# Delta-rule mixer of a decoder step: gate distances on ScalarE, an earlier block inverse, and sample slots in two periods

## What is computed

```
gc = cumsum(g);  decay = exp(gc_i - gc_j) for i >= j, else 0
A = (beta k) k^T * decay below the diagonal;  T = A + I;  solve T u = beta v, T w = beta k exp(gc)
v_new = u - w S;   o = (q exp(gc)) S + (q k^T * decay) v_new
S = S exp(g_last) + (k exp(g_last - gc))^T v_new
```

## Time and profile before

| | us |
|---|---|
| median of 3 runs (3142.27 to 3144.38) | 3142.46 |
| the profiled execution | 3141.53 |
| its span, first to last instruction | 3139.9 |
| PE busy in the span | 3018.0 |
| DVE busy | 1911.0 |
| ACT busy | 1349.6 |
| POOL busy | 186.7 |

### The profile page before, as it was taken

One profiled execution on the slowest core, in us unless ns is written; L12 is line 12 of the kernel. 1 busy time (PEld: TensorE's weight loads), 2 busy tenths in 40 slices (PEclk: granted clock), 3 DMA queues, 4 the chain that ended last, 5 costly groups with the idle time before them and its releaser, 6 DMA issues.

```text
span 3139.9 us, 59809 instructions
## 1 busy us (share of the span) xinstructions
PE 3018.0 (96%) x24010; PEld 2901.5 (92%) x24010; DVE 1911.0 (61%) x2734; ACT 1349.6 (43%) x1970; POOL 186.7 (6%) x227
## 2 busy tenths in 40 slices
PE   6999999999889999999997999999999999999997
PEld 5789999998878999987796999999999999999997
DVE  4644336454676477666369888888888883322224
ACT  5443444334245464434356455555555543212222
POOL 0000000001253000010000000000000001000011
PEclk9999999999999999999998999999999999999998
DMA  7563223332206557886664433333343344433323
GB/s 260 166 214 108 81 76 88 93 94 71 68 28 196 166 183 255 275 322 218 247 207 132 125 120 114 120 114 117 114 120 120 116 128 149 135 96 97 99 93 129
DMA packets 455029, 443.96 MB, mean 141 GB/s; under 512 B 22203, under 2 KB 417740, under 8 KB 446879
## 3 DMA queue, kind: packets, MB, share of 16 engines
q1 hardware_dynamic: 436698, 361.85, 37.4%
q0 software_dynamic: 12416, 69.55, 6.1%
q10 hardware_dynamic: 5776, 10.62, 1.0%
HBM read 408.26 MB, written 33.95 MB: 141 GB/s over the span
## 4 chain that ended last, share of the span: by engine, by line
PE 85%; DVE 7%; ACT 3%; DMA 2%; issue 2%; POOL 1%; ACTq 0%; POOLq 0%; SPq 0%; DVEq 0%
PE ps L2931 17%; PE ps L3330 16%; PE ps L3534 15%; PE ps L3502 9%; PE ps L3504 9%; PE ps L3503 9%; PE ps L2928 4%; DVE w_low L1851 1%; ACT w_high L1118 1%; DMA w_raw<-in_xa_wo 1%; PE ps L3421 1%; DMA q_wide<-q_mid 1%; PE ps L2880 0%; PE ps L3147 0%; DMA w_raw<-in_xa_wk 0%
## 5 line engine op out<-in xcount | busy, mean ns | idle before, releaser
L1851 DVE TENSOR_TENSOR w_low<-w_raw,w_high 128x1024 fp32r<-128x1024 f32 x354 | 435.0, 1229 | 623.0 <-ACT w_high L1118 622.4
L3502 PE MATMUL ps<-set_high,w_hi 128*128 128x260 f32 x2464 | 700.9, 284 | 26.1 <-DVE set_low L2741 19.8
L3504 PE MATMUL ps<-set_high,w_lo 128*128 128x260 f32 x2464 | 700.0, 284 | 0.0
L3503 PE MATMUL ps<-set_low,w_hi 128*128 128x260 f32 x2464 | 699.9, 284 | 0.0
L1118 ACT ACTIVATE w_high<-w_raw 128x1024 fp32r<-128x1024 f32 x356 | 377.2, 1060 | 646.0 <-PE ps L3330 295.1
L3502 PEld LDWEIGHTS ps<-set_high,w_hi 128*128 128x128 f32 x2464 | 467.7, 190 | 29.6 <-DVE set_low L2741 22.6
L3504 PEld LDWEIGHTS ps<-set_high,w_lo 128*128 128x128 f32 x2464 | 468.7, 190 | 0.0
L3503 PEld LDWEIGHTS ps<-set_low,w_hi 128*128 128x128 f32 x2464 | 467.3, 190 | 0.1
L2931 PE MATMUL ps<-x_high,w_high 128*128 128x260 f32 x1568 | 319.7, 285 | 0.2
L2931 PE MATMUL ps<-x_low,w_high 128*128 128x260 f32 x1568 | 315.3, 283 | 0.0
L2931 PE MATMUL ps<-x_high,w_low 128*128 128x260 f32 x1568 | 314.8, 282 | 0.0
(11 more groups left out here) (532 smaller groups left out, 5582.7 us busy)
## 6 DMA issues: line engine op xcount, KB each, us to landing
w_raw<-in_w_in SPq DMA_DIRECT2D x96, 512.0 KB
raw<-in_ffn_w_up SPq DMA_DIRECT2D x176, 256.0 KB, 2.9
raw<-in_ffn_w_gate SPq DMA_DIRECT2D x176, 256.0 KB, 3.2
raw<-in_ffn_w_down SPq DMA_DIRECT2D x176, 256.0 KB, 3.0
w_raw<-in_w_out SPq DMA_DIRECT2D x64, 512.0 KB
w_raw<-in_xa_wq SPq DMA_DIRECT2D x64, 512.0 KB
w_raw<-in_xa_wo SPq DMA_DIRECT2D x64, 512.0 KB
w_raw<-in_xa_wk SPq DMA_DIRECT2D x32, 512.0 KB
```

The lines of the kernel that those rows point to most:

```text
L1851: dve.tensor_tensor(w_low[:, slot], w_raw[:, (g.slab0 + jj) % RAW], w_high[:, slot].bitcast(F32), ALU.subtract).then_inc(sem("w_low_ready" ...
L3502: pe.matmul(ps[:, bank, 0:HALF], high, set_high[:, kp, x], start=kp == 0, stop=False)
L3503: pe.matmul(ps[:, bank, 0:HALF], high, set_low[:, kp, x], start=False, stop=False)
L3504: ins = pe.matmul(ps[:, bank, 0:HALF], low, set_high[:, kp, x], start=False, stop=kp == KP - 1)
```

## The change

Gate distances: DVE's `differ` and `distance` go. ACT makes the absolute distance itself, straight from PSUM, one instruction per head (`far`, with the row's gate as bias and scale -1), and then the exponential as before. POOL clears `s_keys` in DVE's stead. The z GEMM's side work: the reciprocal of the norms goes ahead of a `w_low`; four single broadcasts become two pairs; the blocks' inverse starts one slab earlier and each of its pieces moves up one slab; `s_wide` is made at p = 10 and spread at the second quarter of slab 12, with a wait that ACT has taken block 2, and ACT takes it at p = 12. Chunks: `kk_of` goes to bank 4g, `samples_values` and `samples_step` move on DVE, `sample_keys_turn` goes behind `o_of`. Slots: (1, 0) to (1, 3) and (2, 0) to (2, 3), the first of each period in bank 4g+1. Tail: `o_turn(2)` goes to bank 4g ahead of `state_of`, and `chunk_done(2)` ahead of the last chunk's mean.

First the tables and the wait for `s_wide`, then ACT, then DVE's order in the loop over the chunks, then PE:

```
         WIDE = {(8, 1): (0, 1), (8, 2): (2, 3), (8, 3): (4, 5), (9, 0): (6, 7), (9, 1): (8,), (9, 2): (9,), (9, 3): (10,),
-                (10, 0): (11,), (10, 1): (12,), (10, 2): (13,), (10, 3): (14,), (11, 0): (15,)}
+                (10, 0): (11,), (10, 2): (12, 13), (11, 0): (14, 15)}
...
-        PAIR = {(n, x): u for u, (n, x) in enumerate((n, x) for n, xs in ((0, (4,)), (1, (1, 2, 3, 4)), (2, (1, 2, 3))) for x in xs)}
+        PAIR = {(n, x): u for u, (n, x) in enumerate((n, x) for n in (1, 2) for x in range(4))}
...
-        SLOT_AFTER = {1: ("grow", "differ"), 2: ("inner",), 3: ("k_rows",), 4: ("v_rows",)}
+        SLOT_AFTER = {0: ("inv_t6", 0), 1: ("far", 1), 2: ("far", 1), 3: ("k_rows", 1)}
...
+        def slot_bank(x, g):
+            return 4 * g + (3 if x else 1)
...
+                if p == 12:
+                    act.wait_ge(*after("s_wide_ready", 1))
+                    act.activation(s_bg[:, 0], ps[:, b, 0:BH], ACT.Copy)
+                    act.activation(s_bg[:, 1], ps[:, b, BH:2 * BH], ACT.Exp).then_inc(sem("s_bg_wide"), 1)
...
                 for g in (PREP if n == 0 else range(2)):
-                    act.wait_ge(*step("distance", g, n))
+                    act.wait_ge(*step("grow_ready", g, n))
+                    if n:
+                        act.wait_ge(*step("qk_mask", g, n - 1))
+                    for h in range(HG):
+                        m = n * H + g * HG + h
+                        ins = act.activation(decay[g][:, h], ps[:, 4 * g + 3, h * P:(h + 1) * P], ACT.Abs, bias=gc[:, m:m + 1], scale=-1.0)
+                    ins.then_inc(chunk_sem("far", g), 1)
+                    act.wait_ge(*step("far", g, n))
                     act.activation(decay[g][:], decay[g][:], ACT.Exp, scale=-1.0).then_inc(chunk_sem("decay", g), 1)
```

```
             for n in range(TT - 1):
                 if n:
                     less(n)
-                differ(n + 1)
-                distance(n + 1)
+                else:
+                    samples_values()
+                sample_states(n, 0)
                 if n == 0:
                     samples_taken()
-                    samples_step()
-                if n == 1:
-                    samples_done()
                 sample_states(n, 1)
                 inner_of(n + 1)
+                if n == 0:
+                    samples_step()
                 for g in range(2):
                     state(n, g)
...
                 inverse_of(5, n + 1)
                 if n == 0:
                     samples_rows()
+                if n == 1:
+                    samples_done()
...
-                if (p, k) == (ONE - 1, 1):
-                    pe.wait_ge(*normed(2 * H))
+                if (p, k) == (3 * SL, 1):
+                    pe.wait_ge(sem("acc_taken"), g_z.block0 + 3)
                     pe.wait_ge(*after("s_wide", 1))
...
                 if ahead:
-                    if n:
-                        samples_cleared(n - 1, 4)
+                    samples_beside(n, 0)
                     for g in range(2):
                         grow_of(n + 1, g)
...
                 for g in range(2):
                     v_new(n, g)
-                if ahead:
-                    samples_beside(n, 1)
...
+                samples_cleared(n, 0)
                 for g in range(2):
                     o_of(n, g)
                 if ahead:
-                    samples_cleared(n, 1)
+                    samples_beside(n, 1)
                     for g in range(2):
                         kk_of(n + 1, g)
+                else:
+                    for g in range(2):
+                        pe.wait_ge(*after("o_normed", 3))
+                        o_turn(2, g, 0).then_inc(sem("o_turned"), 1)
```

More of the change, by code:

```diff
@@ L3124, in half_of @@
                     pe.wait_ge(*step("inv_t0", g, n))
[L3125 removed]
+                    if n == 0:
+                        pe.wait_ge(*step("k_rows", g, n))
                 else:
```

155 lines of the change are left out of this document (66 added, 89 removed).

## The result

| | us |
|---|---|
| the changed kernel, median of 4 runs (3119.05 to 3125.4) | 3124.93 |
| before, median of 4 runs beside it (3142.27 to 3144.38) | 3143.22 |
| ratio, 95% interval | 0.9939 [0.9927, 0.9951] |
| the profiled execution, and its span | 3125.4, 3123.5 |
| forecast, and its range | 3123.8, 3118 to 3132 |

The kernel is 18.3 us faster by the medians, 0.6%, and lies inside the range. The profiled executions differ by 16.1 us. Where PE turns the gates' rows, ahead of anything that was changed, the new trace is at 717.73 and the old one at 716.57.

What follows compares the result with a forecast made beforehand. PE was taken to bound nearly everything, so gains up to the w_out GEMM's first matmul pass on whole to the end. The terms summed to -18.7 us, giving a median of 3123.8, range 3118 to 3132.

Steps and rivals of the forecast that it cites:

- The forecast case: Whole kernel: the summed terms hold, 3120.5 to 3128 us, chance 0.66.
- The z GEMM: z GEMM: earlier reciprocal, paired broadcasts, no `s_wide` wait or low clock behind it, less two new waits: -5.6 us.
- The preparation: From the z GEMM's end to `half_of(5, 0)`: released last by the states' load, 10.8 for 16.9 us, -6.0.
- Period 0: Chunk stage's first period: longer by waits at the samples' key turn and `half_t` and a clock drop, +4.8 us.
- That rule of price: New PE waits: priced by the nearest old row, like 2.2 us with a clock drop behind, like 1.9 without.
- period 0 costs little: Rival in period 0: short step passes, ACT's distances overlap `v_new`; -4 us more, 3119.5, chance 0.15.
- Periods 1 and 2: Later chunk periods: slot waits covered and DVE's load lighter, 30.5 and 30.2 us, so -5.9 and -2.4.
- DVE has 4.5 us less: Periods 1 and 2: DVE's work falls by 4.5 us, a pair of distances costing 3.18, of subtractions 1.4.
- The tail: Behind the last period: `chunk_done(2)` leaves the path to `last_turn(0)`, 2.0 earlier there, 1.6 taken: -1.6 us.
- The inverse is not earlier where it counts: Rival in the z GEMM: `w_low` of slab 15 up to 6 us late, PE's clock drops; 3132, chance 0.12.
- ACT holds the chunks: Rival in the chunk stage: ACT holds `grow`, `v_new`, `k_rows`, and 2 us waits return; 3136.5, chance 0.05.
- The clock as a rival: Rival in the chunk stage: spread waits lower PE's clock; 50 such us give 3148.8, 75 give 3161; chance 0.02.

Runs made afterwards that it cites:

- experiment 2: Kernel before with only the gate distances moved to ACT, four Abs activations a group, old order kept: 3163.31 us, ratio 1.0060.
- experiment 1: Kernel before with the z GEMM's part of the change alone: 3136.27 us, ratio 0.9979.
- Experiment 4: Changed kernel with the distances back on DVE in two passes, placed behind slot 0's state updates: 3125.17 us, ratio 0.9943.
- experiment 8: Changed kernel with the second half of the samples' keys moved behind `half_of(5, 0)` on PE: 3125.50 us, ratio 0.9943.
- experiment 6: Changed kernel with the samples' key turn behind chunk 1's key products on PE, and DVE's reading of it behind `inner_of(1)`: 3123.39 us, ratio 0.9933.
- experiment 9: Changed kernel with `s_bg` taken by ACT behind the z GEMM again, ahead of the distances: one run, 3122.43 us.
- experiment 10: Changed kernel with the tail's part undone, chunk 2's `o_turn` and z product back at their old places: one run, 3124.89 us.
- experiment 11: Changed kernel with the split of w_out's fourth slab ahead of the wait for the store of S: 3123.50 us, ratio 0.9935.
- experiment 5: Changed kernel with the next chunk's key products in bank 4g+3 again and the key turn behind `inner`: one run, 3132.1 us.
- experiment 3: Changed kernel with the distances back on DVE in two passes, ahead of slot 0's state updates: 3140.29 us, ratio 0.9993.
- experiment 7: Kernel of experiment 6 with DVE's five passes of the samples' step moved behind `half_of(5, 1)`: 3118.65 us, ratio 0.9918.
- experiment 12: Changed kernel with the changes of experiment 7 and experiment 11 together: 3118.62 us, ratio 0.9922.

## Why the prediction was right or wrong

**The forecast case held**, 1.1 us from the median, and no term is off by more than 0.8. That flatters it: period 0 came out right by errors that cancel, the later periods with one reason that the runs do not bear out and two that the forecast did not have.

*The z GEMM* was 0.8 short. Of the new waits, the one for block 2 was 0.76 for 1.0, but `w_low` of slab 15 was 1.60 for 0.9, and in place of the reciprocal's 1.10 PE waits 0.50 for ACT to take block 1. The slow clock behind the old wait for `s_wide`, 2.5 us of this term, is not there in every execution: experiment 2 had the wait without it. Alone on the kernel before (experiment 1) the part is worth the same 4.9 us, so this term does not hang on the other parts.

*The preparation* is released by the load, as forecast. Only the load was mis-sized: PE got to the second keys 9.7 us behind the GEMM where I had 8.9. Experiment 4 shows that 3.2 of the 5.3 us need the distances on ACT, and experiment 8 that PE has no gap from `half_of(5, 0)` to the inverse's end.

*Period 0*: the sum +4.8 was measured as +4.4, out of terms that were wrong both ways. The turn's wait was 1.87 for 1.6. The wait for `half_t` was 1.25 where I had 3.9, and the clock took 3.2 us where I had 1.5. I had priced the drop behind the long wait; it came behind the short one of 1.87, which I had put at "no drop" by the row of 1.9. That rule of price is the step that failed, and it explains both errors: the slow spell delayed both sides of the later wait: PE ended `k_turn(1)` 19.1 us behind the period's start where I had 15.4, and `half_t` came at 20.4 where I had 19.3. That POOL had stopped when the last two passes ran (3.2 us for the five, where I had 5.6) took 2.4 us off DVE's side, but the passes had begun 3.5 later, at 15.2 for the 11.7 that my sum implies. So the rival "period 0 costs little" has its short passes and not its gain. Where the turn had no wait, in experiments 4 and 6, the forecast's own mechanism is there: 3.81 and 3.80 us for `half_t`, and products of 3.78 behind it.

The kernels of experiments 8 to 11 keep this period 0 and show how the two terms trade: with a slow spell that costs 3.4 us the wait is 1.01, with one that costs 1.7 it is 2.38, and the period is between 29.3 and 29.6 (30.8 in 11, where the products behind the second wait are slow too).

*Periods 1 and 2*: right in size (-5.9 and -2.4 for -6.1 and -2.2), half right in cause. The 1.9 at the slots went in each, as forecast, by the slot ahead of `grow_of`. "DVE has 4.5 us less" is wrong: with those passes back on DVE, behind slot 0, the periods are 30.30 and 30.38. The wait at `kk_of` and its slow clock were in the sum, which left no wait there, but not what removes them: in the kernel before it was `samples_done` ahead of slot 1's updates, and in the new order it is the bank of its own, which is worth 6.8 us (experiment 5) and which the forecast named nowhere. No run moved `samples_done`, or slot 0 on PE, by itself, so the split of the 8.3 us between them is read from the rows of before.

*The tail*: -2.2 at `last_turn(0)` for -1.6, and 2.5 of the 2.8 us that it wins by the fourth slab given back at low clock. "Passed on whole to the end" does not hold for this term, though it does for the rest: from `last_turn(0)` on the two traces differ by 0.4 us.

*The rivals.* "The inverse is not earlier where it counts" was right in kind, 0.7 late at slab 15, and small. "ACT holds the chunks" did not come about, but it is what experiment 2 shows for the same activations in the old order: 3.9 us twice at a slot, 3.7 at the samples' key turn, 3.6 at their keys, and clocks of 0.68 to 0.91 in the three windows, 22 us in all. I gave it 0.05 from ACT's busy share, 17.9 of 36.4, and that share says nothing about it; what excluded it, as I read experiments 2 and 3, was the new order of slots. The clock as a rival stayed small: low in period 0 and behind the tail.

On the Trainium skill's rule ("ScalarE: Activation LUTs", Rules for kernel authors: maxima, sums and products belong on VectorE), this case is a draw. Four Abs took 1.12 to 1.15 us, nearer to the row of 1.14 than to the 1.3 of its cost figures; on DVE the same work gives the same time but for 3.2 us in the preparation. Its rule on the clock ("TensorE: Matmul & The Clock Gate", A second HAM failure mode), that short idle gaps between groups make the clock swing, has more to it here than I allowed: the spell in period 0 stood behind a 1.87 us wait, in each of the six traces that have it.

## What to carry to other kernels

Ask first whose bank, not whose engine. Where several short-lived products pass through one PSUM bank, the engine that reads one of them stands in the queue of the next; here, in the new order, putting one product back into the shared bank cost 7 us, and moving the passes off the busier engine in the old order cost 22. Test a bundled change part by part before believing its reasons, since a sum can be right with the wrong terms in it. What undoing a part costs in the new order need not be what it gained over the old one: look in the old trace too. And do not add a wait and the slow clock ahead of it as if each stood alone, since the slow clock can eat up the wait that follows.

## What the runs showed of the hardware

The same wait does not always bring the same clock. In experiments 7 and 12 period 0 is the same program with the same 1.76 us wait. In one execution the two turns behind it take 1.06 and 1.02 us, in the other 0.60 each, and the periods are 27.55 and 25.91 us. The first turn of each:

```profile
874.39 1.06 PE L3132 MATMUL ps<-ident,inv_t 128*128 128x128 f32 x4
```

```profile
874.12 0.60 PE L3133 MATMUL ps<-ident,inv_t 128*128 128x128 f32 x4
```

The same holds in three other places. The 1.87 us wait at the samples' key turn stands in the traces of the changed kernel and of experiments 5, 8, 9, 10 and 11, with the same work ahead of it in period 0: the 16 small products behind it took 3.35, 1.91, 2.38, 2.40, 2.12 and 1.98 us, so the clock fell almost at once in one and later in the others. The wait for `s_wide`, 2.56 and 2.57 us, had half clock behind it in the trace of before and full clock in that of experiment 2: 6.06 and 3.35 us to the GEMM's end. And the 1.9 us wait ahead of `last_turn(0)` had the first product behind it at 0.36 us in the changed kernel and at 0.57 in experiments 5, 8 and 9.

I take the scatter between executions (3115.16 to 3122.21 in experiment 7) to be partly this; no run shows it for an execution without a trace.

Five DVE passes over 128x64 took 5.7, 4.1 or 3.2 us (experiments 6 and 7 and the changed kernel), according to which of POOL's instructions ran beside them: single ones 1.19 to 1.32 beside those of 1.25 us, 0.96 beside those of 1.02, and 0.21 to 0.23 where none had started. DVE's reads of PSUM, such as `s_new<-ps,s_bg`, took 0.21 in the same time.

The Trainium skill, "SBUF — State Buffer", SBUF: two separate sides, says that DVE with two SBUF inputs and GpSimd reading SBUF take one port pair in turn, each for its whole instruction. The trace agrees: a pass beside POOL lasts about as long as one of POOL's instructions, 1.25 or 1.02 us, and one after POOL has stopped 0.23.
